# Layer kernel: gated unit and convolution tail placed between the last projection blocks, selection divided anew

## The chip, the cores and the metric

One core of one Trainium2 chip. The metric is the device time of one execution in microseconds, the median of the runs. Three runs of the kernel before gave 3154.9, 3154.71 and 3153.0 us, median 3154.71 us. The profiled execution took 3150.2 us, of which 3148.4 us lie between its first and last instruction (the span).

## The reference, cut to what matters

One pre-norm layer of a hybrid encoder, for 2048 prompt tokens and 32 sample tokens with 1024 cached keys. One projection of the normed input to 7748 columns feeds three branches, a gate path and merge gates:

```python
(aq, ak, av, iq, ik, iw, za, uv, zb, glu, zc, gates) = split_columns(rms_norm(x, norm_g) @ w_in)
# A: each query keeps the 256 best visible keys by an indexer score, then softmax attention over them
score = einsum('bths,bth->bts', relu(einsum('bthd,bsd->bths', iq, ik)), iw);  sel = top_k(score, 256)
# B: gmlp_unit
u, v = split(gelu(uv)); v = layer_norm(v, ln_g, ln_b)
o_b = u * (einsum('gij,bnjgc->bnigc', w_masked, v_chunks) + bs)        # chunks of 128 positions, 4 groups
# C: conv_module
c = a * sigmoid(g); y = causal_depthwise_conv31(c) + b; o_c = silu(layer_norm(y, ln_g, ln_b))
merged = ga*((o_a*silu(za)) @ w_a) + gb*((o_b*silu(zb)) @ w_b) + gc*((o_c*silu(zc)) @ w_c)
x = x + merged @ w_out;  x = x + sigmoid(rms_norm(x) @ w_pg) * (p @ w_ple);  y = rms_norm(x)
```

All of it is float32; matmuls run as three products of a high and a low part.

## The kernel before, in words

`STAGES` runs in this order on every engine: constants, trunk, gmlp, attend_loads, swish, turnover, attend, merge, finish.

**Trunk** (`stage_trunk`). The projection is cut into 61 jobs (`JOBS`) of 128 columns. A job is 5 spans of 416 tokens, a span is 8 slices (one for each 128 rows of the weights), a slice is 3 matmuls. After a span ScalarE copies or activates the PSUM bank into one of two buffers `j_out` and issues a store to `T_dram` (`evacuate`): five stores in a job. `high` (ScalarE) and `low` (GpSimd) split the next job's weights. Between these, ScalarE and GpSimd work through the depthwise convolution in 20 units (`make` and `add`), from job 9 on, spread over `CONV_JOBS` jobs by `CONV_TIMES`. From job 18 on one tile of keys and values a job is turned and stored (`natural_load`, `natural_store`).

**Selection** (`stage_select`), inside the trunk. The 256th best score of each row is found by bisection in two halves of 16 steps: the upper 16 bits, then the lower. For a tile in `DVE_TILES` VectorE does both (`whole`). For a tile in `ACT_TILES` VectorE prepares the keys (`offer`), ScalarE searches the upper half with sign sums (`Search.step`, L399), and VectorE does the rest (`complete`: waits for `found`, then `finish`, which ends at L455). The order on VectorE is written out by hand. When ScalarE takes a search step is fixed at build time by a planner in `scalar`: from the due time in `ACT_DUE`, whenever its running account of free time (`room`, from `JOB_US`, `EVACUATE_US`, `TAP_US`) covers half a step; at most half a job is saved up. The first step of a tile waits for `offer`. SyncE stores finished tiles and loads the next ones in the order of `FINISHED` and `LOADED`, and moves convolution units in between (`units`), also by planned times.

**Gmlp** (`stage_gmlp`) starts when all trunk stores and the selection are done. The values are loaded whole (`g_vT`), turned to token-major (L584), measured (L630), the mixing weights turned, then for each of 17 tiles: turned again, normed (L636), mixed (L600), shifted (L651), and GpSimd multiplies u by z (L697) and the result by that (L700). ScalarE's queue stores `g_ob`, two buffers.

**Swish** (`stage_swish`) works on the convolution's output `c.y`, loaded whole: for 5 spans of 422 columns, column sums by a ones matmul (L1362), centring (L1387), squares (L1417), sums of squares; then once over 2110 columns a square root, a reciprocal and one correction; then norm, silu and gate in 4 groups.

**Attend loads** put keys, values and the caches into rows of the attention's score buffer. SyncE issues them inside swish. **Turnover** waits for all engines and clears the semaphores. **Attend** first turns the cached keys, splits all operands into high and low (L1737, L1775), and TensorE starts on the first scores when every split is done (`operands`). The queries of tile 0 are loaded after the turnover and split by GpSimd (L1624 to L1628).

## Time and profile before

| stretch of the span, us | what | PE busy | granted clock |
|---|---|---|---|
| 0 to 1570.3 | trunk, 61 jobs | 80 to 100% of each 100 us or more | 0.97 to 1.00 |
| 1570.3 to 1776.6 | gmlp, swish, turnover | 80.4 of 206.3 | 0.73 |
| 1776.6 to 1799.7 | attention's operands | 3.3 of 23.1 | 0.57 |
| 1805 to 2352 | attention | 515.3 of 547.0 | 0.99 |
| 2352 to 2658 | merge | 277.1 of 306.0 | 0.94 |
| 2658 to 3148 | finish | 442.6 of 490.0 | 0.95 |
| 3148.4 | span | 2823.3 | 0.957 |
| 3150.2 | profiled execution | | |
| 3154.71 | median of three runs | | |

PE is TensorE. Busy is the time in which at least one matmul runs; granted clock is the share of full speed. The lines below name a source line, an engine, the tiles written and read, the shapes and how often. A bracket after a line of the timeline is the idle time before it and what ended it.

### The profile page before, as it was taken

What the parts mean: (1) busy time and instruction counts of PE and PEld (TensorE: products, weight loads), DVE (VectorE), ACT (ScalarE), POOL (GpSimd) and SP (SyncE); (2) the same over time, 40 slices, a digit from 0 to 9 for tenths busy, and PEclk for the clock granted to TensorE, in tenths of its full rate; (3) what the DMA queues carried; (4) which work ended last, traced back from release to release, by engine and by line L of the source; (5) the groups of instructions that cost most, each with busy time, mean ns of one, the idle gap of its engine ahead of it and who ended that gap; (6) DMA issues with size and microseconds to landing.
All of it is one profiled execution on the core that took longest, in us unless ns stands there. A gap on an engine that the chain in (4) does not pass through costs nothing. (4 is left out here: it accounts for less than half of the span.)

```text
span 3148.4 us, 43098 instructions
## 1 busy us (share of the span) xinstructions
PE 2823.3 (90%) x14677; PEld 2581.2 (82%) x14677; DVE 2302.5 (73%) x4035; ACT 1608.9 (51%) x2672; POOL 1342.9 (43%) x926
## 2 busy tenths in 40 slices
PE   6999999999999998898945189999988997799998
PEld 6999999999999998898942167778868897688886
DVE  7478947729999999999654778889976465465554
ACT  5375677877776767677201377777761001211111
POOL 1100477777888685676331254332213342111110
PEclk9999999999999999999987599999999998899999
DMA  4434233232333232232275332211016456311110
GB/s 152 127 130 154 69 105 106 91 121 92 104 114 103 82 121 83 76 108 67 89 239 134 116 74 55 67 54 41 30 35 218 152 161 216 97 65 65 65 65 34
DMA packets 293850, 321.07 MB, mean 102 GB/s; under 512 B 37537, under 2 KB 267681, under 8 KB 290077
## 3 DMA queue, kind: packets, MB, share of 16 engines
q1 hardware_dynamic: 158013, 180.90, 18.8%
q10 hardware_dynamic: 135648, 137.80, 13.2%
q8 instruction: 100, 1.64, 0.2%
q14 instruction: 89, 0.73, 0.1%
HBM read 194.46 MB, written 123.48 MB: 101 GB/s over the span
## 5 line engine op out<-in xcount | busy, mean ns | idle before, releaser
L1171 PE MATMUL psum<-hT_hi,j_whi 128*128 128x416 f32 x2440 | 868.1, 356 | 37.3 <-ACT j_out L1044 28.3
L1171 PE MATMUL psum<-hT_hi,j_wlo 128*128 128x416 f32 x2440 | 860.3, 353 | 0.0
L1171 PE MATMUL psum<-hT_lo,j_whi 128*128 128x416 f32 x2440 | 859.3, 352 | 0.0
L823 POOL TENSOR_TENSOR v_y<-v_y,v_product 128x422 f32<-128x422 f32 x580 | 721.1, 1280 | 246.9 <-ACT v_product L809 246.7
L1171 PEld LDWEIGHTS psum<-hT_hi,j_whi 128*128 128x128 f32 x2440 | 461.3, 189 | 54.2 <-ACT j_out L1044 32.8
L1171 PEld LDWEIGHTS psum<-hT_lo,j_whi 128*128 128x128 f32 x2440 | 462.5, 190 | 11.3
L1171 PEld LDWEIGHTS psum<-hT_hi,j_wlo 128*128 128x128 f32 x2440 | 461.6, 189 | 5.5
L416 DVE TENSOR_SCALAR_CACHE_REDUCE s_high<-s_key,s_cand 128x1024 int16<-128x1024 f32 (+4 forms) x240 | 392.9, 1637 | 8.4
L809 ACT ACTIVATE v_product<-v_x,v_taps 128x422 f32<-128x422 f32 x580 | 339.6, 640 | 74.2 <-POOL v_y L823 34.6
L1003 POOL TENSOR_TENSOR j_wlo<-j_w,j_whi 128x1024 fp32r<-128x1024 f32 x61 | 154.3, 2530 | 269.2 <-ACT j_whi L1036 269.1
L1803 DVE TENSOR_TENSOR a_ptlo<-psum,a_pthi 128x512 fp32r<-128x512 f32 x338 | 227.1, 681 | 45.3 <-ACT a_pthi L1752 44.8
L399 ACT ACTIVATE s_ajunk<-s_high,s_abias 128x2048 uint8<-128x2048 uint16 (+2 forms) x135 | 232.4, 1722 | 46.8 <-ACT j_out L1044 46.0
L1752 ACT ACTIVATE a_pthi<-psum 128x512 fp32r<-128x512 f32 x338 | 190.9, 595 | 111.6 <-PE psum L1687 110.1
L1044 ACT ACTIVATE j_out<-psum 128x416 f32<-128x416 f32 x305 | 153.2, 502 | 153.6 <-PE psum L1171 129.4
L1744 ACT ACTIVATE a_l<-a_l,a_lows 128x512 f32<-128x512 f32 (+4 forms) x136 | 183.7, 1351 | 38.1 <-DVE a_lows L1787 36.3
L1952 PE MATMUL psum<-m_ohi,m_whi 128*128 128x416 f32 x480 | 170.5, 355 | 30.1 <-POOL m_olo L1937 30.1
L1687 PEld LDWEIGHTS psum<-ident,a_l 128*128 128x128 f32 x1352 | 164.3, 140 | 40.6 <-ACT a_l L1744 4.4
L1713 PE MATMUL psum<-a_khi,a_qs 128*128 128x512 f32 x320 | 152.9, 478 | 47.0 <-DVE a_lows L1787 23.2
L1687 PE MATMUL psum<-ident,a_l 128*128 128x128 f32 x1352 | 192.5, 273 | 2.2 <-ACT a_l L1744 2.0
L2121 POOL TENSOR_TENSOR f_mhi<-f_mraw,zero 128x1024 fp32r<-128x1024 f32 x17 | 32.2, 1893 | 374.4 <-DMA f_mraw<-M_dram 333.9
L1952 PE MATMUL psum<-m_ohi,m_wlo 128*128 128x416 f32 x480 | 171.2, 357 | 0.0
L1952 PE MATMUL psum<-m_olo,m_whi 128*128 128x416 f32 x480 | 169.4, 353 | 0.0
(284 smaller groups left out, 5351.5 us busy)
## 6 DMA issues: line engine op xcount, KB each, us to landing
T_dram<-j_out ACTq DMA_DIRECT2D x305, 208.0 KB, 1.9
j_w<-in_w_in ACTq DMA_DIRECT2D x59, 512.0 KB, 4.1
m_gate<-T_dram SPq DMA_DIRECT2D x60, 416.0 KB, 3.5
m_oraw<-B_dram SPq DMA_DIRECT2D x15, 832.0 KB, 6.6
SC_dram<-i_acc SPq DMA_DIRECT2D x40, 256.0 KB, 2.0
M_dram<-m_merged ACTq DMA_DIRECT2D x5, 1664.0 KB, 10.4
n_x<-in_x_prompt SPq DMA_DIRECT2D x16, 512.0 KB, 4.6
a_q<-T_dram SPq DMA_DIRECT2D x32, 256.0 KB, 4.6
```

The costliest lines, as they stand in the source:

```text
L399: do(act.activation(a_junk[:, 0:n], high[HIGH_HALF[t]][:, 0:n], ACT.Sign, bias=bias, accum_out=a_cnt[:]))
L416: do(vec.tensor_scalar(junk, src, cand[:], 0.0, ALU.is_ge, ALU.add, accum_out=cnt[:]))
L809: act.activation(product[n % RING][:], x_in[:, k:k + CW_SPAN], ACT.Identity, scale=taps[:, k:k + 1]).then_inc(made, 1)
L823: pool.tensor_tensor(y[n % 2][:], y[n % 2][:], product[n % RING][:], ALU.add).then_inc(added, 1)
L1003: pool.tensor_tensor(w_lo[j % 2][:], w_raw[:], f32(w_hi[j % 2][:]), ALU.subtract).then_inc(w_lo_done, 1)
L1044: act.activation(out[r][:], c.psum[:, bank_of(j, b), 0:SPAN], FUNC[JOBS[j][2]]).then_inc(bank_read, 1)
L1171: last = pe.matmul(bank, w[p][:, k, :], h[:, k, t0:t0 + SPAN], start=(k == 0 and q == 0), stop=(k == KD - 1 and q == 2))
L1687: last = pe.transpose(c.psum[0:w, PT[u], r * P:(r + 1) * P], L[h][:, kt * P:kt * P + w], c.ident[:])
L1744: act.activation(L[h][:, 0:n], L[h][:, 0:n], ACT.Exp, bias=lows[:, h, lowest:lowest + 1], scale=-1.0, accum_out=sums[:, h:h + 1]).then_inc ...
L1752: act.activation(pT_hi[u][0:w, :], c.psum[0:w, PT[u], :], ACT.Copy).then_inc(pt_hi, 1)
L1803: vec.tensor_tensor(pT_lo[u][0:w, :], c.psum[0:w, PT[u], :], f32(pT_hi[u][0:w, :]), ALU.subtract).then_inc(pt_free[u], 1)
L1952: last = pe.matmul(c.psum[:, n, 0:SPAN], wt[:, b, k, n * P:(n + 1) * P], o[u][:, k, :], start=(k == 0 and q == 0), stop=(k == 3 and q == 2))
```

## The change

- `STAGES` is now constants, trunk, turnover, attend, merge, finish. Gmlp and swish are called inside the trunk: TensorE's part slice by slice from `span` (`gmlp.tensor_in`, `swish.tensor_in`), GpSimd's at the end of a job, ScalarE's after an evacuation, VectorE's after the selection, SyncE's after the selection's stores.
- Gmlp has a slice of its own for each step from job 56, span 4 (`GMLP_FROM`), swish a span for each half step from job 58, span 2 (`SWISH_FROM`). The values are loaded tile by tile into a ring of four, and twice. Stores go by SyncE. Swish takes its square root by `rsqrt` (14 small VectorE operations) for each span of 422.
- The attention gate's four silu jobs become the last four.
- Five stores of a job become two (`HELD`), from five buffers.
- Selection: 8 tiles for ScalarE, 7 for VectorE (tile DT goes over), in turn; new due times; `EVACUATE_US` 0.95 to 0.72; the convolution is spread over 47 jobs, not 49.
- Raw keys are loaded during swish, raw values and caches after its stores. Attention waits for fewer splits before its first score; the others follow (`splits` on VectorE in its first group, `late_split` on GpSimd before group 4).

Constants, the order of the jobs and the selection:
```diff
-        + [(col + s * P, slot + s, "silu") for col, slot in ((C_ZB, S_ZB), (C_ZC, S_ZC), (C_ZA, S_ZA)) for s in range(4)]
-        + [(C_G + s * P, S_G + s, "sigmoid") for s in range(24)])
+        + [(col + s * P, slot + s, "silu") for col, slot in ((C_ZB, S_ZB), (C_ZC, S_ZC)) for s in range(4)]
+        + [(C_G + s * P, S_G + s, "sigmoid") for s in range(24)]
+        + [(C_ZA + s * P, S_ZA + s, "silu") for s in range(4)])
...
-OUTS = 2
+HELD = [(0, 2), (2, 5)]
+GATED_UNIT_STORED = 29
+SWISH_GATE_STORED = 33
...
-CONV_FROM, CONV_JOBS = 9, 49
+CONV_FROM, CONV_JOBS = 9, 47
+GMLP_FROM, SWISH_FROM = (56, 4), (58, 2)
...
-JOB_US, EVACUATE_US, TAP_US, HIGH_US, SCORE_US = 22.8, 0.95, 0.66, 1.2, 0.455
+JOB_US, EVACUATE_US, TAP_US, HIGH_US, SCORE_US = 22.8, 0.72, 0.66, 1.2, 0.455
...
-ACT_TILES = [12, 13, 14, 15, 8, 9, 10, 11, DT]
-DVE_TILES = [4, 5, 6, 7, 2, 3]
-ACT_DUE = [32.0, 117.0, 212.0, 331.0, 546.0, 704.0, 846.0, 962.0, 1076.0]
-LOADED = [(12, 0), (4, 1), (13, 2), (14, 1), (15, 0), (5, 2), (8, 1), (6, 2), (9, 0), (7, 2), (10, 1), (2, 2), (11, 0), (3, 2), (DT, 1)]
-FINISHED = [(4, 98), (12, 193), (13, 311), (14, 453), (5, 529), (15, 610), (6, 686), (8, 753), (7, 829), (9, 895), (2, 945), (10, 1011),
-            (3, 1060), (11, 1125), (DT, 1169)]
-HIGH_HALF = {4: 0, 12: 1, 13: 0, 14: 1, 15: 0, 5: 1, 8: 1, 6: 0, 9: 0, 7: 1, 10: 1, 2: 0, 11: 0, 3: 1, DT: 1}
+ACT_TILES = [12, 13, 14, 15, 8, 9, 10, 11]
+DVE_TILES = [4, 5, 6, 7, DT, 2, 3]
+ACT_DUE = [30, 115, 277, 437, 595, 754, 870, 986]
...
-        whole(DVE_TILES[1])
-        for x in range(3, 7):
+        for x in range(len(ACT_TILES) - 1):
             offer(x + 1)
             complete(x)
-            whole(DVE_TILES[x - 1])
-        offer(8)
-        complete(7)
-        complete(8)
-    c.selected = [(early_stored, 32)] + [(s, 16 * sum(x == k for x in slot.values())) for k, s in enumerate(stored)]
+            if x + 1 < len(DVE_TILES):
+                whole(DVE_TILES[x + 1])
+        complete(len(ACT_TILES) - 1)
```
Gmlp, SyncE's part:
```diff
+    def sync(sp, rest_of_units):
+        c.wait_for_stored(sp, GATED_UNIT_STORED - 1)
+        c.wait_for_selected(sp)
...
+        def load_v(n):
+            t, r = n % TILES, n % RING
+            if n >= RING:
+                sp.wait_ge(turned, n - RING + 1)
+            sp.dma_start(vT[r][:, :, 0:real(t)], slot(S_GV, t)).then_inc(v_full[r], 16)
+        def load_uz(t):
+            p = t % 2
+            if t >= 2:
+                sp.wait_ge(gated, t - 1)
+            sp.dma_start(zT[p][:, :, 0:real(t)], slot(S_ZB, t)).then_inc(uz_full[p], 16)
+            sp.dma_start(uT[p][:, :, 0:real(t)], slot(S_U, t)).then_inc(uz_full[p], 16)
+        def store(t):
+            sp.wait_ge(gated, t + 1)
+            sp.dma_start(c.B_dram[1, :, :, at(t)].rearrange("s q t -> q s t"), ob[t % 2][:, :, 0:real(t)]).then_inc(stored[t % 2], 16)
+        for n in range(RING):
+            load_v(n)
+        load_uz(0)
+        load_uz(1)
+        rest_of_units(float("inf"))
+        for n in range(RING, TILES + RING):
+            load_v(n)
+        for t in range(TILES):
+            if TILES + RING + t < 2 * TILES:
+                load_v(TILES + RING + t)
+            store(t)
+            if t + 2 < TILES:
+                load_uz(t + 2)
+        sp.wait_ge(normed, TILES)
+        sp.dma_start(c.O["gmlp_sample"], vn[DT % 2][0:DEC].rearrange("q g n -> q (g n)")).then_inc(v_stored, 16)
+        sp.wait_ge(v_stored, 16)
+        for p in range(2):
+            sp.wait_ge(stored[p], 16 * len(range(p, TILES, 2)))
```
Gmlp, TensorE's part (`turn` turns four blocks of 128 by 128, `second` turns a tile again, after the norm of tile t - 2), and VectorE's and GpSimd's:
```diff
+    def mix(pe, t):
+        rows = real(t)
+        pe.wait_ge(normed, t + 1)
+        if t:
+            pe.wait_ge(mix_read, t)
+        for g in range(4):
+            last = pe.matmul(c.psum[:, MIX, g * P:(g + 1) * P], vn[t % 2][0:rows, g, :], wT[0:rows, g, :], start=True, stop=True)
+        last.then_inc(mixed, 1)
...
+        n = (j * len(SPANS) + b) * KD + k - first_slice
+        if 0 <= n < TILES:
+            if n == 0:
+                c.wait_for_natural(pe)
+            if n >= 3:
+                pe.wait_ge(measured, n - 2)
+            turn(pe, n, 5 + n % 3)
+        elif n == WEIGHTS_AT:
...
+        elif n == AGAIN_AT:
+            second(pe, 0)
+        elif AGAIN_AT < n <= AGAIN_AT + 2 * TILES:
+            t, odd = divmod(n - AGAIN_AT - 1, 2)
+            if odd:
+                mix(pe, t)
+            elif t + 1 < TILES:
+                second(pe, t + 1)
...
+        def shift(t):
+            p = t % 2
+            vec.wait_ge(mixed, t + 1)
+            if t >= 2:
+                vec.wait_ge(stored[p], 16 * (t // 2))
...
+        norm(0)
+        for t in range(TILES):
+            if t + 1 < TILES:
+                norm(t + 1)
+            shift(t)
...
+    def gates_in(pool, j):
+        for t in range(TILES):
+            if (first_slice + AGAIN_AT + 2 + 2 * t) // (KD * len(SPANS)) != j:
+                continue
+            p, w = t % 2, real(t)
+            pool.wait_ge(uz_full[p], 32 * (t // 2 + 1))
+            pool.tensor_tensor(uT[p][:, :, 0:w], uT[p][:, :, 0:w], zT[p][:, :, 0:w], ALU.mult).then_inc(multiplied, 1)
+            pool.wait_ge(multiplied, t + 1)
+            pool.wait_ge(mix_read, t + 1)
+            pool.tensor_tensor(ob[p][:, :, 0:w], ob[p][:, :, 0:w], uT[p][:, :, 0:w], ALU.mult).then_inc(gated, 1)
```
Swish:
```diff
+    def load_gate(sp, x):
+        if x:
+            sp.wait_ge(gated, x)
...
+    def sync(sp):
+        c.wait_for_moved(sp)
+        load(sp, 0)
+        load(sp, 1)
+        c.wait_for_gated(sp)
+        c.wait_for_stored(sp, SWISH_GATE_STORED - 1)
+        load_gate(sp, 0)
+        load(sp, 2)
...
+        x, odd = divmod(j * len(SPANS) + b - first_span, 2)
+        if (x, odd, k) == (X, 0, 0):
+            turn_tails(pe)
+        if not 0 <= x < X:
+            return
+        if not odd and k == 0:
+            if x == 0:
+                c.wait_for_mixed(pe)
+                pe.wait_ge(ones_made, 1)
+            else:
+                pe.wait_ge(centred, x)
+            pe.wait_ge(y_full[x % YS], 16 * (x // YS + 1))
+            total(pe, SUM, y[x % YS], summed)
+        if odd and k == 3:
+            pe.wait_ge(squared, x + 1)
+            if x >= 2:
+                pe.wait_ge(var_read, x - 1)
+            total(pe, 6 + x % 2, squares, var_summed)
...
+        def norm(x):
+            vec.wait_ge(var_summed, x + 1)
+            vec.tensor_scalar(var[:], c.psum[:, 6 + x % 2, 0:CW_SPAN], EPS, None, ALU.add).then_inc(var_read, 1)
+            vec.wait_ge(var_read, x + 1)
+            rsqrt(steps, rstd[:], var[:], tmp[:])
+            wide = rstd[:].unsqueeze(1).to_broadcast([P, 4, CW_SPAN])
+            vec.tensor_tensor(y[x % YS][:], y[x % YS][:], wide, ALU.mult).then_inc(normed, 1)
...
+        for x in range(X):
+            centre(x)
+            norm(x)
+            if x:
+                gate(x - 1)
...
+    def scalar_in(act, j, b):
+        x, odd = divmod(j * len(SPANS) + b - first_span, 2)
+        if 0 <= x < X and not odd:
+            act.wait_ge(centred, x + 1)
+            if x:
+                act.wait_ge(var_summed, x)
+            act.activation(squares[:], y[x % YS][:], ACT.Square).then_inc(squared, 1)
+        if odd and 0 <= x - 1 < X:
+            swish(act, x - 1)
```
Trunk:
```diff
-        select.sync(sp)
+        units = select.sync(sp)
+        gmlp.sync(sp, units)
+        swish.sync(sp)
+        load_keys.keys(sp)
+        swish.stores(sp)
+        load_keys.values(sp)
...
+            elif j == 2:
+                act.wait_ge(stored[r], 32)
+            else:
+                act.wait_ge(stored[1 if b < 2 else 4], 16 * j)
+            act.activation(out[:, r, :], c.psum[:, bank_of(j, b), 0:SPAN], FUNC[JOBS[j][2]]).then_inc(bank_read, 1)
+            if j < 2:
+                act.wait_ge(bank_read, q + 1)
+                act.dma_start(c.T_dram[slot, :, t0:t0 + SPAN], out[:, r, :]).then_inc(stored[r], 16)
+            elif b in (1, 4):
+                first, end = HELD[0 if b == 1 else 1]
+                act.wait_ge(bank_read, q + 1)
+                act.dma_start(c.T_dram[slot, :, first * SPAN:end * SPAN], out[:, first:end, :].rearrange("q b t -> q (b t)")
+                              ).then_inc(stored[b], 16)
...
-        while search.left():
-            search.step()
-        act.wait_ge(kv_stored, 32 * TILES)
+        assert not search.left()
+        wait_for_stored(act, SLOTS - 1)
```
Attention:
```diff
+            if group.n == 4:
+                for n in range(len(late_splits)):
+                    late_split(n)
...
+    splits = [(ks_hi[g][:, 0:PAST], ks_lo[g][:, 0:PAST], cacheT[g], (cache_turned, 1)) for g in range(KVH)]
+    splits += [(k_hi[g][:], k_lo[g][:], kraw[g][:], (k_full, 128)) for g in range(KVH)]
     for g in range(KVH):
-        splits += [(k_hi[g][:], k_lo[g][:], kraw[g][:], (k_full, 128)),
-                   (ks_hi[g][:, 0:PAST], ks_lo[g][:, 0:PAST], cacheT[g], (cache_turned, 1)),
-                   (ks_hi[g][:, PAST:], ks_lo[g][:, PAST:], new_k[g], (k_full, 128))]
-    for full, n, v, raw, rows, tiles in ((v_full, 16, v_p, vraw, P, slice(0, DT)),
-                                         (vs_full, 32, v_s, vsraw, P, slice(0, NV - 1)),
-                                         (vs_full, 32, v_s, vsraw, DEC, slice(NV - 1, NV))):
-        for g in range(KVH):
-            src, dst = raw[0:rows, tiles, g * HD:(g + 1) * HD], v[0:rows, tiles, g, :]
-            splits.append((dst[:, :, 0:HD], dst[:, :, HD:P], src, (full, n)))
+        for x in range(2):
+            dst = v_p[:, x * (DT // 2):(x + 1) * (DT // 2), g, :]
+            splits.append((dst[:, :, 0:HD], dst[:, :, HD:P], vraw[x][:, :, g * HD:(g + 1) * HD], (v_full, 32)))
+    FIRST_KEYS, FIRST_VALUES = KVH + 1, 2 * KVH + 2
...
-        pe.wait_ge(operands, 1)
...
+                if group.t == 0:
+                    pe.wait_ge(operands, FIRST_KEYS + group.g)
+                if group.t == DT:
+                    pe.wait_ge(late_ready, len(late_splits))
...
+            if group.n == 0:
+                for n in range(FIRST_KEYS, len(splits)):
+                    split(n)
```

## Rows read from the trace of the kernel before

**Rows 1.** Windows: length, PE, PEld, DVE, ACT, POOL busy, granted clock, DMA share, GB/s.
```profile
1570.30:1776.60 206.30, 80.39 (x377) 55.41 (x377) 105.80 (x154) 21.73 (x14) 41.86 (x35) 0.73 0.59 175
...
1620.00:1660.00 40.00, 18.57 (x140) 15.98 (x141) 22.14 (x59) 0.00 (x0) 28.82 (x24) 1.00 0.86 231
...
1660.00:1684.70 24.70, 5.28 (x22) 4.32 (x21) 7.54 (x16) 0.00 (x0) 7.74 (x8) 0.50 0.92 244
...
1776.60:1799.70 23.10, 3.26 (x16) 3.02 (x16) 20.57 (x12) 10.30 (x13) 17.35 (x14) 0.57 0.57 114
```
**Rows 2.** Timeline of PE: start and length in us, line, tiles, shapes, count.
```profile
1569.93 0.35 PE L1171 MATMUL psum<-hT_hi,j_wlo 128*128 128x416 f32 x1
...
1650.98 1.16 PE L600 MATMUL psum<-g_wT,g_vn 128*128 128x128 f32 x8 [1.43 <-DVE g_vn L636]
1651.98 0.60 PE L584 MATMUL psum<-ident,g_vT 128*128 128x128 f32 x4
...
1697.34 3.00 PE L1362 MATMUL psum<-g_y,w_ones 128*128 128x422 f32 x8
...
1799.74 0.80 PE L1713 MATMUL psum<-a_khi,a_qs 128*128 128x512 f32 x1 [19.89 <-DVEq L1776]
```
**Rows 3.** The page's part 5: the projection's weight loads.
```profile
L1171 PEld LDWEIGHTS psum<-hT_hi,j_whi 128*128 128x128 f32 x2440 | 461.3, 189 | 54.2 <-ACT j_out L1044 32.8
```
**Rows 4.** Waits from 300 to 1571 us: in total, times, longest.
```profile
DVE s_high L442 <- ACT s_afound L405: 141.8, 3, 60.4
...
ACT s_ajunk L399 <- DVEq L466: 47.6, 4, 15.9
```
**Rows 5.** Timeline of DVE in the selection: first finish, and ends of tiles.
```profile
446.76 1.61 DVE L442 TENSOR_SCALAR s_high<-s_high,s_afound 128x2048 bf16<-128x2048 uint16 x1 [42.05 <-ACT s_afound L405]
...
865.38 0.75 DVE L455 SCALAR_TENSOR_TENSOR s_key<-s_iota,s_qtail,s_key 128x512 f32<-128x512 int16 x1
...
947.67 1.47 DVE L455 SCALAR_TENSOR_TENSOR s_key<-s_iota,s_qtail,s_key 128x512 f32<-128x512 int16 x1
...
1028.16 1.48 DVE L455 SCALAR_TENSOR_TENSOR s_key<-s_iota,s_qtail,s_key 128x512 f32<-128x512 int16 x1
...
1186.35 0.75 DVE L455 SCALAR_TENSOR_TENSOR s_key<-s_iota,s_qtail,s_key 128x512 f32<-128x512 int16 x1
...
1250.41 1.46 DVE L455 SCALAR_TENSOR_TENSOR s_key<-s_iota,s_qtail,s_key 128x512 f32<-128x512 int16 x1
...
1546.75 0.75 DVE L455 SCALAR_TENSOR_TENSOR s_key<-s_iota,s_qtail,s_key 128x512 f32<-128x512 int16 x1
```
**Rows 6.** DMA issues in the gmlp and swish stages: KB each, median us to landing.
```profile
w_gate<-T_dram SPq DMA_DIRECT2D x4, 1040.0 KB, 6.8
...
g_uT<-T_dram SPq DMA_DIRECT2D x13, 256.0 KB, 3.8
B_dram<-g_ob ACTq DMA_DIRECT2D x13, 256.0 KB, 4.0
```
**Rows 7.** Timelines of POOL, DVE and ACT in the gmlp and swish stages.
```profile
1652.00 1.27 POOL L697 TENSOR_TENSOR g_uT<-g_uT,g_zT 128x512 f32<-128x512 f32 x1 [0.84 <-DMA g_uT<-T_dram]
...
1656.55 1.13 DVE L651 SCALAR_TENSOR_TENSOR g_ob<-psum,g_gain,g_offset 128x128 f32<-128x128 f32 x4 [1.70 <-DMA B_dram<-g_ob]
...
1690.70 1.91 DVE L1387 TENSOR_TENSOR g_y<-g_y,psum 128x1688 f32<-128x1688 f32 x1 [19.54 <-PE psum L1362]
...
1692.73 1.61 ACT L1417 ACTIVATE w_squares<-g_y 128x1688 f32<-128x1688 f32 x1 [121.90 <-DVE g_y L1387]
...
1738.75 2.36 DVE L1396 TENSOR_TENSOR w_tmp<-w_tmp,w_rstd 128x2110 f32<-128x2110 f32 x1
1741.14 1.26 DVE L1397 TENSOR_SCALAR w_tmp<-w_tmp 128x2110 f32<-128x2110 f32 x1
```
**Rows 8.** Timelines of SP and POOL after the turnover.
```profile
1776.55 0.67 SPq L159 DMA_DIRECT2D a_q<-T_dram  x1
...
1788.00 3.43 POOL L1628 TENSOR_TENSOR a_qs<-a_q,a_qs 64x1024 fp32r<-64x1024 f32 x1
```

574 lines of the change are left out of this document (278 added, 296 removed).

## The prediction

> **What bounds the kernel now.** I read the windows first, then TensorE's timeline, the waits, and VectorE's timeline through the selection. The reader is to see four things.
>
> The projection ends at 1570.3 us [rows 2]. From there to the attention's first scores at 1799.7 [rows 2] lie 229.4 us in which TensorE has little to do: 80.4 us busy of 206.3, then 3.3 of 23.1 [rows 1]. This is the only large stretch that the change can give back. Attention, merge and finish are not touched, so I move them as a block.
>
> The projection itself is TensorE's. A weight load takes 189 ns [rows 3] and is paced with its matmul, so a slice of three is 0.567 us, a span 4.54 and a job 22.7 us. Work put between slices adds its whole TensorE time, and every wait of TensorE there too, since TensorE takes its instructions in order.
>
> VectorE's selection ends at 1547.5 [rows 5], 22.8 us before the projection. 141.8 us of its length are three waits for ScalarE's searches, and ScalarE in turn waited four times for VectorE, 47.6 us in all [rows 4].
>
> Between 1620 and 1660 the gmlp stage is bound by neither compute engine: TensorE is busy 18.6 of 40 us, GpSimd 28.8, while the DMA engines are busy for 0.86 of it at 231 GB/s [rows 1]. A tile takes 3.45 us there. It is a ring of two buffers: a store lands after 4.0 us [rows 6], then VectorE's shift 1.13 and GpSimd's 1.27 [rows 7], plus 0.5 for the issue and hand-overs, 6.9 us for two tiles.
>
> **The change part by part.** I follow the moment at which TensorE can go on, from the selection to the first scores.
>
> *Selection.* With tiles in turn, VectorE no longer waits except for the first search, which ended at 446.8 [rows 5]. Its 16 steps are spread over spans by the planner's account; 0.23 us more room a span and one span earlier start bring the end to span 3 of job 12 from span 1 of job 13, three spans or 13.6 us. I take 432. From there VectorE works without a gap. Durations by differences of the ends of tiles [rows 5]: prepare one and complete one of 2048 keys 82.3 us (865.4 to 947.7), a whole tile of 1024 80.5 (947.7 to 1028.2), one of 1536 64.1 (1186.4 to 1250.4). A whole tile of 512 and one of 1056 lie around them; I take 63 and 76. Sum: 432 + 75 (finish tile 12) + 3 x 80.5 + 3 x 82.3 + 76 + 3 x 64 + 2 x 63 + 60 (last finish) = 1449. That is 98 us sooner than 1547.5. Without the first wait it would be 20 less; if ScalarE's late searches are not done in time, 15 more. ScalarE may still wait for `offer` around tiles 10 and 11 and hold TensorE up as now, but TensorE must then wait for the selection anyway: without any hold-up job 56, span 4 would begin near 1412, with those of before at 1462. So VectorE's chain sets the start, and lost projection time before it costs nothing.
>
> *Stores and room.* Three issues of a store fewer a job free ScalarE, about 1.2 us; the planner spends this on the searches. It is off the path: 0, bounds -5 and +3.
>
> *Start of gmlp.* SyncE stores the last tile (landing 3), issues four constants of 256 KB and the first values; landing behind them 6. I take 13 us: first turn at 1462. Bounds 8 and 20: before the last store SyncE also waits for the last convolution unit, which GpSimd should end near the same 1450.
>
> *Gmlp between slices.* It covers 61 slices, 34.6 us of projection. TensorE's own addition: 34 turns of four at about 0.5 (0.60 with its tail), 17 mixes of 1.0 [rows 2], with the constants 2: 36 us. But the waits decide. First pass: 17 turns, each needs 256 KB; with the gates' loads of 1 MB ahead of the fifth, at 231 to 270 GB/s, 24 us instead of 18. Nine slices without tiles and the small VectorE work: 7. Second pass: each mix waits for the shift before it, and that for a store two tiles back. Now the store, z and u are issued in a row by SyncE after GpSimd's product, so the ring is 0.15 + 3 x 0.37 issue + 4.3 landing + 1.27 + 1.27 + 0.3 = 8.4 us for two tiles, and the tile's DMA is 1024 KB where it was 768: at 231/0.86 = 269 GB/s at least 3.9 us. I take 4.5 us a tile (bounds 2.6, TensorE's own two slices, a turn and a mix, and 5.4, the DMA share of before scaled). 17 x 4.5 = 77. Together 24 + 7 + 77 = 108 us: last mix at 1570.
>
> *Start of swish.* It comes three slices later, but TensorE waits for `y_full`, and SyncE loads y only after the last tile is stored and `gmlp_sample` has landed. Last mix, shift and product 2.5, two landings of small stores 3.5, issue 0.5, y of 864 KB below the 6.8 of 1040 KB [rows 6], say 5.5: 12 us (bounds 8, 17). First column sum at 1582.
>
> *Swish.* Thirteen spans, 59.0 us. TensorE adds ten sums of 2.84 (3.00 with the tail [rows 2]) and 1.2 for the tails: 29.6. VectorE's loop is longer. Between one sum of squares and the next: `norm` (0.6 + 14 small operations on 422 columns, by the 2110-column rows 2.36/5 and 1.26/5 plus fixed parts [rows 7] about 0.5 and 0.3 each, 7.1 in all, + 1.91) = 9.6; `gate` 1.91; `centre` 1.91 [rows 7]; square 1.61 [rows 7]; the sum 2.84 and a slice boundary 0.5. That is 18.4 against TensorE's 2 x 4.54 + 2 x 2.84 = 14.8. The first sum of squares comes 9.7 after the start because the square is queued behind ScalarE's evacuation; four loops 73.6; 2.84 + five slices 2.84; tails 1.2; three spans 13.6: 104 us. Bound from below 90 if the loop is hidden, above 115. Projection ends at 1686, against 1570.3.
>
> *Turnover.* VectorE gates the last span just as TensorE ends; then store (landing 6), the tails' stores, and SyncE's issues of caches and values, about 7. Attention starts 15 us after the projection (bounds 10, 22): 1701. Before it was 206.3.
>
> *First scores.* Now the queries bound: q is issued at 1776.55 and its last split ends at 1791.43 [rows 8], 14.9 us. Keys and values were loaded before, and only three splits precede. I take 14. First score at 1715, against 1799.7. In the first group VectorE must still do five splits (2.3 + 4 x 1.1 us) before the first reciprocal: +6.5. GpSimd's six late splits, some 8 us, lie beside an attention in which TensorE is busy 94% and GpSimd a third: 0, at most +5.
>
> The move of the four silu jobs costs nothing: the same 61 jobs.
>
> Sum: 1799.7 - 1715 - 6.5 = 78 us saved. The profiled execution of 3150.2 becomes 3072; against the median of 3154.7, 4.5 us above it, 3077.
>
> By the clock: between 1620 and 1660, TensorE less than half busy with turns and mixes, the clock stayed at 1.00, that is at 2.4 GHz; between 1660 and 1684.7, busy a fifth, it was 0.50, at 1.2 GHz [rows 1]. In the changed gmlp phase TensorE is busy 2.6 us of 4.5, more than in the first of these. The Trainium skill (TensorE: Matmul & The Clock Gate, Part 4: PE-mode transpose) says that turning does not count as TensorE's activity for the clock; taken strictly, the second pass could run at 1.2 GHz. The first window speaks against it, the mixes being a part of it.
>
> **Rivals.**
> *Waits hidden.* The ring of stores and VectorE's loop in swish stay below TensorE's own work. Then gmlp takes 34.6 + 36 = 71 instead of 108, swish 92 instead of 104: another 49 us, 3028. For it: the stores of before landed in 4.0 with loads in between. Against it: GpSimd alone needs 2.54 a tile and its ring held TensorE idle half the time [rows 1]. Chance 0.14.
> *Late start or low clock.* The selection or the last convolution unit comes 20 us late, or the clock falls in the gmlp phase (slices 1.13, turns and mixes double: 5.2 a tile and 2.1 a turn, +24), or loads queue: 3098 to 3112. For it: ScalarE and VectorE wait for each other [rows 4] and the new due times leave 9 us. Chance 0.26.
> *The ring swallows it.* SyncE issues values, stores and gates in one order. If a landing of u or y is then two or three times 4 us, since all of it goes through one queue, each mix holds the whole projection. From 4.5 + 78/17 = 9.1 us a tile on, the change loses; at 10 us it is 3170. For it: 0.92 DMA share at 244 GB/s when other loads joined [rows 1]. Against it: 9.1 us are two landings in series and 1 MB needs 3.9. Chance 0.04.
> *It doesn't do what it says.* TensorE reaches span 4 of job 56 long before the selection, and all of gmlp and swish comes as late as now: within 0.2% of 3155. Chance 0.02.
>
> **How the numbers follow.** The forecast has 0.54 and its own range is 3052 to 3096 (the bounds of the terms, added as independent). The range of 8 in 10 reaches over most of the late case and a part of the hidden one: 3040 to 3112. A difference under 0.2%, 6 us, is what a measurement here cannot tell from none. Faster 0.94, same 0.02, slower 0.04.
>
> **What would show it.** The last L455 near 1449 with only one wait for `s_afound`; the first turn of gmlp at 1462; mixes 4.5 us apart, waiting for VectorE, that for `B_dram<-g_ob`; sums of squares 18.4 apart, waiting for ScalarE's squares; the last projection matmul at 1686; the first score at 1715. I am wrong if mixes follow each other every 2.6 us, if the projection before gmlp loses more than now, or if the turnover comes later than 22 us after the last slice.

## The result: 36 us faster, and where the other 42 went

Four executions of the changed kernel took 3114.23, 3118.1, 3117.54 and 3123.77 us, median 3117.82; the kernel before has a median of 3154.14 over four. The ratio is 0.9887, interval 0.987 to 0.9904: 36 us or 1.1% faster, beyond the noise, but less than half of the gain that I forecast (3077), and just above the range, whose end was 3112. The profiled execution took 3114.23 us, its span is 3112.2 against 3148.4.

The milestones, by the steps of the prediction:

| moment | predicted | measured | what lies between, predicted / measured |
|---|---|---|---|
| first cut of ScalarE found | 432 | 434.6 | |
| selection ends | 1449 | 1488.7 | 1017 / 1054.1 |
| first turn of gmlp | 1462 | 1500.5 | 13 / 11.8 |
| last mix | 1570 | 1597.2 | 108 / 96.7 |
| first column sum of swish | 1582 | 1608.2 | 12 / 11.0 |
| projection ends | 1686 | 1719.7 | 104 / 111.4 |
| attention's first turn | 1701 | 1737.9 | 15 / 18.2 |
| first score | 1715 | 1753.4 | 14 / 15.5 |

From the first score to the last instruction the changed kernel takes 10.2 us more than the one before (6.5 predicted). So 39.7 us of the miss stand before gmlp, and behind it -1.2 - 11.3 - 1.0 + 7.4 + 3.2 + 1.5 + 3.7 = +2.3 us.

TensorE's timeline, the lines that answer to [rows 2]:

```profile
1500.51 1.09 PE L603 MATMUL psum<-ident,g_vT 128*128 128x128 f32 x4 [16.60 <-DMA g_vT<-T_dram]
...
1536.17 1.09 PE L619 MATMUL psum<-g_wT,g_vn 128*128 128x128 f32 x8
...
1597.16 1.12 PE L619 MATMUL psum<-g_wT,g_vn 32*128 32x128 f32 x8 [3.09 <-DVEq L682]
1608.20 4.56 PE L814 MATMUL psum<-w_y,w_ones 128*128 128x422 f32 x6 [6.19 <-DMA w_y<-Y_dram]
...
1719.30 0.35 PE L1421 MATMUL psum<-hT_hi,j_wlo 128*128 128x416 f32 x1
1737.85 3.68 PE L1807 MATMUL psum<-ident,a_cache 128*128 128x128 f32 x16 [18.20 <-POOLq L2389]
1753.35 0.79 PE L1847 MATMUL psum<-a_khi,a_qs 128*128 128x512 f32 x1 [11.82 <-POOL a_qs L1741]
```

TensorE reached the first slice of the gmlp unit at 1483.9 and stood there for 16.6 us, because the values are loaded only after the last tile of the selection is stored. This wait takes the place of TensorE's idle time in the separate stages of before.

The waits from 300 to 1500 us (total, times, longest), which answer to [rows 4]:

```profile
DVE s_high L439 <- ACT s_afound L402: 42.4, 2, 31.0
ACT s_ajunk L396 <- DVEq L463: 32.5, 4, 17.4
...
PE psum L1452 <- DMA t_kvT<-T_dram: 20.7, 6, 7.5
...
PE psum L1421 <- ACT j_out L1288: 15.7, 3, 11.4
```

VectorE's wait for ScalarE fell from 141.8 to 42.4 us as intended: 31.0 for the first cut, and 11.4 for the last, which I had at zero. Windows of the gmlp stage's second pass, the swish and the turnover (columns as in [rows 1]):

```profile
1533.70:1598.30 64.60, 47.24 (x294) 39.95 (x293) 33.73 (x82) 3.12 (x5) 41.78 (x32) 0.95 0.89 245
1608.20:1719.70 111.50, 98.01 (x397) 77.35 (x397) 66.78 (x91) 27.91 (x39) 2.34 (x1) 0.92 0.43 134
1719.70:1737.90 18.20, 0.05 (x1) 0.05 (x1) 1.95 (x2) 0.51 (x1) 0.00 (x0) 0.56 0.90 233
```

TensorE was busy 80.4 of 206.3 us in the old stages [rows 1]; now it is 47.2 of 64.6 us in the second pass and 98.0 of 111.5 in the swish. DMA is as dense in the second pass as it was (0.89 at 245 GB/s against 0.86 at 231), in the swish it is not (0.43). The granted clock of the second pass is 0.95, near the upper level of 2.4 GHz: with projection slices between them, turns and mixes did not bring it down. Turns alone were not run.

### The profile page after: what moved, and what is told of

Read it like the earlier page. It is cut to its first block and busy times, and to the rows that moved or that the text cites. A ratio compares the mean times of both kernels' runs of the same rounds, so it can differ in the third digit from the quotient of the medians.

```text
span 3112.2 us, 42780 instructions
## 1 busy us (share of the span) xinstructions
PE 2835.6 (91%) x14677; PEld 2585.5 (83%) x14677; DVE 2343.5 (75%) x4162; ACT 1573.1 (51%) x2618; POOL 1369.7 (44%) x936
## 5 line engine op out<-in xcount | busy, mean ns | idle before, releaser
L1421 PE MATMUL psum<-hT_hi,j_whi 128*128 128x416 f32 x2440 | 880.2, 361 | 28.9 <-ACT j_out L1288 15.7
L1051 POOL TENSOR_TENSOR v_y<-v_y,v_product 128x422 f32<-128x422 f32 x580 | 737.2, 1310 | 197.3 <-ACT v_product L1037 197.2
L1421 PEld LDWEIGHTS psum<-hT_hi,j_whi 128*128 128x128 f32 x2440 | 464.5, 190 | 47.2 <-ACT j_out L1288 22.1
L413 DVE TENSOR_SCALAR_CACHE_REDUCE s_high<-s_key,s_cand 128x1024 int16<-128x1024 f32 (+4 forms) x240 | 393.0, 1637 | 8.4
L1241 POOL TENSOR_TENSOR j_wlo<-j_w,j_whi 128x1024 fp32r<-128x1024 f32 x61 | 161.7, 2651 | 321.0 <-ACT j_whi L1275 320.8
L396 ACT ACTIVATE s_ajunk<-s_high,s_abias 128x2048 uint8<-128x2048 uint16 (+1 forms) x120 | 214.1, 1784 | 13.2 <-ACT j_out L1288 12.1
L1880 ACT ACTIVATE a_l<-a_l,a_lows 128x512 f32<-128x512 f32 (+4 forms) x136 | 183.7, 1351 | 30.5 <-DVE a_lows L1929 28.8
```

The source lines that it names most:

```text
L396: do(act.activation(a_junk[:, 0:n], high[HIGH_HALF[t]][:, 0:n], ACT.Sign, bias=bias, accum_out=a_cnt[:]))
L413: do(vec.tensor_scalar(junk, src, cand[:], 0.0, ALU.is_ge, ALU.add, accum_out=cnt[:]))
L1051: pool.tensor_tensor(y[n % 2][:], y[n % 2][:], product[n % RING][:], ALU.add).then_inc(added, 1)
L1241: pool.tensor_tensor(w_lo[j % 2][:], w_raw[:], f32(w_hi[j % 2][:]), ALU.subtract).then_inc(w_lo_done, 1)
L1421: last = pe.matmul(bank, w[p][:, k, :], h[:, k, t0:t0 + SPAN], start=(k == 0 and q == 0), stop=(k == KD - 1 and q == 2))
L1880: act.activation(L[h][:, 0:n], L[h][:, 0:n], ACT.Exp, bias=lows[:, h, lowest:lowest + 1], scale=-1.0, accum_out=sums[:, h:h + 1]).then_inc ...
```

## The experiments

All edits are to the changed kernel unless another is named. "Selection's end" is the end of the last tile's L452, "the stretch" the time from the first turn of gmlp (L603) to attention's first turn (L1807): 237.3 us in the changed kernel. Each run has one profile, so such moments are those of one execution; medians are over all executions. The runs were made on several chips, each beside the kernel before, whose medians lie between 3153.2 and 3156.0; the ratios allow for that, differences of medians do not.

**The start follows the selection.** First, both units (gmlp and swish) start a span later.

```diff
-GMLP_FROM, SWISH_FROM = (56, 4), (58, 2)
+GMLP_FROM, SWISH_FROM = (57, 0), (58, 3)
```

> The changed kernel with the gated unit's slices and the swish's slices both one span of the projection later (GMLP_FROM (57, 0), SWISH_FROM (58, 3)). In the changed kernel TensorE reached the unit's first slice at 1483.9 us and waited 16.6 us there. Theory A (TensorE's own idle time sets the end): the wait shrinks by one span, 4.6 us, and the total by 4 to 5 us, to about 3109.5 us. Theory B (VectorE's chain from the end of selection to the swish's last gate sets the end, TensorE follows): the first turn of a tile stays within 2 us of 1500.5, the last projection matmul comes some 4 us earlier, the turnover stays near 1737.5, and the total moves by less than 1.5 us.

Ratio 0.9904 (0.9887 to 0.992), median 3124.0. TensorE's wait did not become a gain: it is 14.0 us instead of 16.6, and the stretch is 238.4 us. Selection ended 5.9 us later (1494.6), although nothing in it was changed, and the first turn (1506.8) moved with it. So theory B's chain holds and A fails; B's own numbers, a first turn within 2 us of 1500.5 and a total within 1.5, were missed mostly by these 5.9 us, whose cause is an instruction shown below.

```diff
-            search(K, e, 1)
+            search(K, e, 1, 1)      # the last of 16 steps left out
```

(`search` gets a fourth argument for it, 0 elsewhere.)

> The changed kernel with the last of the 16 steps of the low-half search left out in each of the 15 searched tiles (the cut found is then off by one step). A step is 2.35 us at 2048 keys, 1.81 at 1536, 1.28 at 1024, 0.75 at 512 and about 0.6 us of small instructions: 34 us less on VectorE in all. Theory A (VectorE's chain is what was late, and it also held TensorE back, because ScalarE stood 29.7 us in front of tiles that VectorE had not offered yet and read out no banks meanwhile): TensorE reaches the unit's first slice 15 to 30 us before 1483.9, the first turn comes 20 to 34 us before 1500.5, and the total falls by 18 to 34 us. Theory B (TensorE is late by stalls of its own): TensorE still reaches the slice at about 1484, the wait of 16.6 us goes and nothing more, total 12 to 17 us shorter. Theory C (ScalarE's last search sets the end of selection): its end stays near 1436, selection ends only some 3 us sooner and the total falls by 3 us.

0.9825 (0.9803 to 0.9847), median 3100.2. Selection ended at 1469.9, the first turn came at 1482.3, 18.2 us sooner, and the total fell by 17.6. That is theory A, though just under its ranges (20 and 18 us), for of 34 us less work only 19 arrived in selection's end. TensorE reached the first slice at 1465.2, 18.7 us sooner. What is gained in selection's end reaches the total nearly one to one.

**What made the selection long.**

```diff
-            pool.tensor_tensor(y[n % 2][:], y[n % 2][:], product[n % RING][:], ALU.add).then_inc(added, 1)
+            half = CW_SPAN // 2
+            pool.tensor_tensor(y[n % 2][:, 0:half], y[n % 2][:, 0:half], product[n % RING][:, 0:half], ALU.add).then_inc(added, 1)
```

> The changed kernel with GpSimd's 560 additions of the convolution over half of their columns (the other half of each product is left out of the sum). One add of 128x422 takes 1.31 us; half should take about 0.7, so GpSimd is some 340 us less busy between 320 and 1440 us. Theory A (VectorE's slow tiles come from work beside GpSimd): pieces of selection fall from 83.0 and 86.7 us per tile to about 80.5 and 82.3 us as I had summed, the single instructions that took 1555 ns (128x512 multiply of the tops) and 1421 ns (signs) fall to about 1080 and 990 ns, selection ends 20 to 30 us sooner, total 15 to 25 us shorter. Theory B (the sizes of the pieces were summed wrongly and GpSimd has no part in them): pieces change by less than 1 us, total by less than 5 us, from ScalarE's waits for the adds alone (52.5 us).

0.9674 (0.9657 to 0.9691), median 3053.3: 64.6 us less, three times what I expected. (This kernel leaves out half of the convolution's sum, so its result is not the layer's.) Selection ended at 1428.9, 60 us sooner, though VectorE now waits 41 us for the last cut. VectorE's groups between 320 and 1440 us, of the changed kernel and then of this run:

```profile
L413 DVE TENSOR_SCALAR_CACHE_REDUCE s_high<-s_key,s_cand 128x2048 int16<-128x2048 f32 x64 | 150.2, 2346 | 2.2
L450 DVE TENSOR_SCALAR s_key<-s_iota,s_qfrom 128x512 f32<-128x512 int16 x37 | 47.2, 1275 | 1.3
L426 DVE TENSOR_SCALAR s_high<-s_key 128x1024 int32<-128x1024 int32 x14 | 21.4, 1530 | 0.1
```

```profile
L413 DVE TENSOR_SCALAR_CACHE_REDUCE s_high<-s_key,s_cand 128x2048 int16<-128x2048 f32 x64 | 150.2, 2347 | 2.2
L450 DVE TENSOR_SCALAR s_key<-s_iota,s_qfrom 128x512 f32<-128x512 int16 x40 | 29.6, 740 | 1.4
L426 DVE TENSOR_SCALAR s_high<-s_key 128x1024 int32<-128x1024 int32 x14 | 15.2, 1089 | 0.1
```

The searching instruction (L413) costs the same to a nanosecond; the others pay for GpSimd's additions. Adding up, for each line and form, the time above the shortest instruction of that line and form, from 300 to 1550 us, gives 128 us in the kernel before, 127 in the changed one, 70 here. So the price is large, but it was in the kernel before as well.

```diff
-            for x, (a, w) in enumerate(pieces(n)):
-                do(vec.tensor_scalar(K[:, a:a + w], iota[:, 0:w], -1.0, q_from[:, x, t:t + 1], ALU.mult, ALU.add))
+            for a in range(0, n, WIDE):          # WIDE = 1536, iota_wide has as many columns
+                w = min(WIDE, n - a)
+                do(vec.tensor_scalar(K[:, a:a + w], iota_wide[:, 0:w], -1.0, q_from[:, a // PIECE, t:t + 1], ALU.mult, ALU.add))
```

> The changed kernel with an iota of 1536 instead of 512 columns, so that the distances of a tile are written by one or two instructions instead of up to four: 21 instead of 46 over the searched tiles (the junk row of tile 16 lies on the buffers of the k and v tiles, long done by then). In the changed kernel this instruction took from 0.49 to 1.67 us for the same 512 columns, 30.4 us above its shortest in all, and the run with half of the additions cut that to 10.8 us. Theory A (each such instruction waits for an addition of GpSimd's under way, a price per instruction rather than per column): VectorE's chain shortens by 15 to 25 us and the total by as much. Theory B (the price is per column: both engines share the bandwidth while they overlap): 512 columns cost the same in a wide instruction, VectorE gains 0 to 5 us, and so does the total.

(The wide row needs room: the junk row of tile 16 moved onto other buffers, with a wait for those in front of that tile.) 0.9831 (0.9815 to 0.9848), median 3101.6, 16.3 us less, which is A's number. Selection ended at 1476.6, 12.1 us sooner; the rest lies behind it. Its groups:

```profile
L453 DVE TENSOR_SCALAR s_key<-s_iota,s_qfrom 128x1536 f32<-128x1536 int16 x7 | 13.5, 1923 | 0.2
L453 DVE TENSOR_SCALAR s_key<-s_iota,s_qfrom 128x1024 f32<-128x1024 int16 x4 | 5.9, 1476 | 0.1
L453 DVE TENSOR_SCALAR s_key<-s_iota,s_qfrom 128x512 f32<-128x512 int16 x6 | 5.8, 967 | 0.2
```

1536 columns cost 1.92 us where three pieces cost 3.8 (3 x 1.275): the price beside additions is mostly per instruction.

**The instructions of 6 to 22 us.** In the profile of every kernel without gaps, the one before included, but not in the one with half additions, VectorE had one to three of them, scans (L446, 5.2 to 6.6 us) left aside. They are always L439 or L445 (by the changed kernel's lines), the first full-width instructions after a search. The largest, in the run with two Newton rounds (below), and GpSimd beside it:

```profile
883.09 22.14 DVE L439 TENSOR_SCALAR s_high<-s_high,s_cand 128x1024 bf16<-128x1024 uint16 x1
905.26 2.00 DVE L440 SCALAR_TENSOR_TENSOR s_key<-s_key,s_high 128x1024 f32<-128x1024 uint16 x1
```

```profile
880.42 14.77 POOL L1051 TENSOR_TENSOR v_y<-v_y,v_product 128x422 f32<-128x422 f32 x14
895.16 2.39 POOL L1241 TENSOR_TENSOR j_wlo<-j_w,j_whi 128x1024 fp32r<-128x1024 f32 x1
897.52 7.43 POOL L1051 TENSOR_TENSOR v_y<-v_y,v_product 128x422 f32<-128x422 f32 x7
905.02 1.16 POOL L1055 TENSOR_TENSOR v_yout<-v_y,v_y 128x422 f32<-128x422 f32 x1
```

It began beside a row of 14 additions and lasted through the subtraction (L1241) and seven more. It ended at 905.23; GpSimd's row had ended at 904.95 and its next instruction began 0.07 us later. In the run a span later L439 took 17.57 us for tile 16, 16.1 more than in the changed kernel's profile; tile 16 ended 12.6 us later there, and the next piece gave 6.8 us back: that is its late selection. The other form did not help:

```diff
-            do(vec.tensor_scalar(above, H[:, 0:n], threshold, 65536.0, off, ALU.mult))
+            do(vec.scalar_tensor_tensor(out=above, in0=H[:, 0:n], scalar=threshold, in1=factors[:, 0:1].to_broadcast([P, n]), op0=off, op1=ALU.mult))
```

(and the same for `is_equal`, L445)

> The changed kernel with two of VectorE's instructions in each finish (the shift of the upper half to bfloat16, and the comparison for equality into int16) written as scalar_tensor_tensor with a constant as second tensor, the same result. In the runs so far single ones of just these two took 6 to 22 us instead of 0.5 to 1.6 (22.14 us in one run, 17.57 in another, 8.2 in nearly all), each time beside a chain of GpSimd's additions without a gap, and none did with the additions halved. Theory A (this form of instruction is kept out as long as GpSimd has additions in a row, others only for one addition): no instruction of VectorE except scans takes over 4.5 us in selection; the new forms cost about 1 us more each at 2048 keys, 15 us in all, so selection ends between 5 us sooner and 8 us later than 1488.7, the runs scatter less. Theory B (any instruction of VectorE can be hit): others of 6 to 20 us appear, and selection ends 15 us later.

0.9982 (0.9965 to 0.9999), median 3144.8: a miss of theory A, and the nine executions scatter more, not less (3136.7 to 3161.5). The same two places still took 9.06 and 7.39 us, no others did (so not B either), and the new form costs more everywhere: at 2048 keys 2.81 us on average in L439's place, where it was 1.21, and 2.91 in L445's, where it was 1.59. Selection ended at 1516.0. A second form at the same places is hit as well; whether the place alone decides was not tested. Then gaps for GpSimd:

```diff
-                pool.wait_ge(added, u * ADDED + (n - 1))
+                pool.wait_ge(added, u * ADDED + n)
```

> The changed kernel with every addition of GpSimd's chain waiting for the addition just before it to be complete, instead of the one before that, so that a small gap stands after each (the sums are the same). In the changed kernel additions in a row follow each other every 1.06 us without a gap. Single instructions of VectorE took 6 to 22 us beside them, always the first full-width ones after a search, in whichever form; each ended within 0.2 us of the last addition of a row. Theory A (VectorE gets in only where GpSimd leaves a gap): no instruction of VectorE apart from scans takes over 4.5 us; selection ends 10 us or more before the usual 1489 to 1506, near 1470 to 1480, and the total is 3098 to 3112 us. Theory B (the gap makes GpSimd's chain longer, ScalarE wait for it, and so TensorE): selection ends as before or later and the total is 3120 us or more. Theory C (gaps do not matter; the first instruction after a search is slow for another reason): 6 to 20 us instructions stay.

> As the run with a gap after each addition, but a gap only after every fourth. Theory A: a starved instruction waits for at most four additions, 4.3 us, so none takes over 6 us; other instructions stay as in the changed kernel; selection ends 5 to 12 us before the usual, total 3103 to 3114 us. Theory B and C: as in the run with a gap after each; under B this one costs a quarter of that one.

(for the second, `n` where `n % 4 == 0`, else `n - 1`.) Gap after each: 0.9884 (0.9869 to 0.9899), median 3119.4; after every fourth: 0.986 (0.9845 to 0.9875), 3113.0. The mechanism of A is borne out: L439 and L445 took at most 3.13 us, nothing but scans more than 4.4. The gain is not: selection ended at 1497.1 and 1491.4, and the time above the shortest is 131 and 125 us, about the 127 of the changed kernel. What the long ones no longer take, the short ones do. So these instructions move selection's end from one profile to the next, by 5.9 us in the run a span later, but they are not the miss. That they make the scatter of the executions is not shown here: it is 6.9 and 8.2 us with gaps against 9.5 without.

**ScalarE's side.**

```diff
-ACT_DUE = [30, 115, 277, 437, 595, 754, 870, 986]
+ACT_DUE = [30, 115, 284, 437, 595, 768, 892, 1002]
```

> The changed kernel with four of ScalarE's eight searches due later (tile 14 by 7 us, 9 by 14, 10 by 22, 11 by 16), so that ScalarE is not sent in front of a tile that VectorE has yet to offer. In the changed kernel it stood there four times, 32.5 us in all, and read out no banks meanwhile. Theory A (VectorE's chain sets the start of the units, and projection time lost before it costs nothing): the four waits shrink below 10 us in sum, TensorE reaches the unit's first slice 10 to 25 us earlier and waits there as much longer than 16.6 us, and selection's end and the total stay as they are, within what the starved instructions of VectorE scatter them (some 8 us). Theory B (these waits are what the missing time is): the total falls by 15 us or more.

0.992 (0.9905 to 0.9935), median 3128.9: slower by 11 us, neither theory. TensorE did wait 37.1 us at the first slice, 20.5 more than in the changed kernel, but it got there no sooner (1487.3). ScalarE's waits stayed at 30.2 us; two instructions of 17.58 and 16.66 us (L439) held VectorE up, and selection ended at 1511.9. The profiled execution (3138.1) is the slowest of the four; the others took 3128.1 to 3129.3, so some 10 us of the loss have no profile. That a late selection moves the total is seen once more: the stretch is unchanged (236.9). Whether later due times help without such a mishap is not shown.

```diff
+        whole(DVE_TILES[-1])        # tile 3, now between complete(10) and complete(11)
         complete(len(ACT_TILES) - 1)
```

(with the last whole tile left out of the loop, the key buffers of tiles 3 and 11 exchanged and tile 11 due 54 us earlier)

> The changed kernel with the last tiles in another order: tile 11 is offered to ScalarE before tile 10 is completed, VectorE's own tile 3 comes after that, and tile 11 is completed last as before; tile 11's search is due 54 us earlier, tiles 11 and 3 exchange key buffers. In the changed kernel VectorE waited 11.45 us for the last cut. Theory A (this wait is in the chain that starts the units): it goes, selection ends 9 to 13 us sooner (near 1477), the first turn still 12 us behind it, total 8 to 13 us shorter. Theory B (TensorE cannot be at the unit's first slice before 1484, and ScalarE's denser searching takes away from the projection what VectorE gains): the first turn comes at 1495 or later and the total falls by less than 5 us.

0.9879 (0.9863 to 0.9896), median 3116.2: 1.7 us less, B's number but not its reason, since TensorE still waits 15.1 us at the first slice. The wait for the last cut is gone, and VectorE waits for no other engine after the first cut; but from the end of tile 9 to selection's end it takes 183.7 us instead of 187.9, and a 13.1 us instruction (L439, tile 16) came before. The prepare of tile 11 now falls beside additions and takes 10.6 us instead of 5.1, and other instructions are moved beside them too. Of 11.45 us of waiting 4.2 arrived.

**The kernel before with the new selection alone** (tile lists, junk row, due times, `EVACUATE_US`; the scratch for DMA descriptors is halved to 4096 bytes to make room).

> The kernel before with nothing changed but the selection: tiles alternate between ScalarE and VectorE as in the changed kernel, tile 16 is searched by VectorE with a junk buffer of its own, ScalarE's due times and evacuation cost are those of the changed kernel (and the scratch for DMA descriptors is 4096 bytes, to make room). Theory A (the new order of selection shortens VectorE's chain, but in the kernel before the projection ends last): selection ends near 1450 to 1490 instead of 1546.75, the last projection matmul stays between 1560 and 1575 (1569.93 before), and the total changes by less than 10 us either way. Theory B (the long search on ScalarE was what held back the last projection jobs as well): the projection ends 20 to 30 us sooner, and so does the kernel, so that selection alone carries most of the 36 us.

1.0055 (1.0038 to 1.0072), median 3172.4: slower by 16.6 us, and both theories wrong. Selection ends 41.7 us sooner (1505.8), but the projection ends 18.9 us later (1588.8). TensorE's waits from 300 to 1500 us are, before and here:

```profile
PE psum L1171 <- ACT j_out L1044: 28.3, 7, 9.6
PE psum L1200 <- DMA t_kvT<-T_dram: 10.3, 3, 6.4
PE psum L1171 <- POOL j_wlo L1003: 4.3, 4, 2.1
```

```profile
PE psum L1163 <- ACT j_out L1036: 22.2, 10, 11.5
PE psum L1163 <- POOL j_wlo L995: 17.1, 8, 5.3
PE psum L1192 <- DMA t_kvT<-T_dram: 14.7, 5, 6.3
```

That is 11 us more; the rest I cannot assign. One candidate was not tested: the planner's `EVACUATE_US` of 0.72 belongs to two stores a job, and this kernel still issues five, so ScalarE may be sent to search when it should read out banks. TensorE's waits for ScalarE's read-outs came 10 times instead of 7 but are shorter in sum; those for GpSimd's split of the weights, which follows ScalarE's, grew from 4.3 to 17.1 us. What the run shows is that an earlier selection alone gains nothing, because in the kernel before the projection ends last.

**The swish's loop.**

```diff
-            rsqrt(steps, rstd[:], var[:], tmp[:])
+            rsqrt(steps, rstd[:], var[:], tmp[:], 2)      # rounds, 3 before
```

> The changed kernel with two rounds instead of three in the swish's inverse square root (4 of VectorE's 14 small instructions a tile left out, in the swish alone; the result is less exact). In the changed kernel the sums of squares stand 20.5 us apart, 5 of them; a round is 0.60 + 0.60 + 0.38 + 0.60 us and the steps between, 2.32 us. Theory A (from the end of selection on VectorE's chain sets the time, and every microsecond of the swish's loop counts five times): the loop falls to 18.2 us and the total by 10 to 12 us. Theory B (TensorE's projection spans fill the loop in any case): the loop stays at 20 us and the total within 2 us.

0.9874 (0.9852 to 0.9896), median 3117.2, as much as the changed kernel. But selection ended 16.8 us late (1505.5, with the 22 us instruction), and the stretch is 221.5 us, 15.8 shorter. ScalarE's squares of the changed kernel and then of this run:

```profile
1634.96 1.61 ACT L894 ACTIVATE w_squares<-w_y 128x1688 f32<-128x1688 f32 x1 [2.08 <-DVE w_y L857]
1655.46 1.61 ACT L894 ACTIVATE w_squares<-w_y 128x1688 f32<-128x1688 f32 x1 [3.85 <-DVE w_y L857]
1675.97 1.61 ACT L894 ACTIVATE w_squares<-w_y 128x1688 f32<-128x1688 f32 x1 [3.85 <-DVE w_y L857]
```

```profile
1649.68 1.62 ACT L894 ACTIVATE w_squares<-w_y 128x1688 f32<-128x1688 f32 x1 [0.47 <-ACT j_out L1288]
1666.20 1.61 ACT L894 ACTIVATE w_squares<-w_y 128x1688 f32<-128x1688 f32 x1 [1.54 <-DVE w_y L857]
```

20.5 us apart against 16.5 (the others 15.4 to 19.1). The swish's loop behaves as theory A has it, and more; the total does not, for the selection was late. 2.3 us less work took more than that from the loop; I read this as the sums' fixed slices, of which a later one is caught or missed, but did not test it.

```diff
+        centre(0)
         for x in range(X):
-            centre(x)
-            norm(x)
+            if x + 1 < X:
+                centre(x + 1)
             if x:
                 gate(x - 1)
+            norm(x)
```

> The changed kernel with VectorE's order in the swish turned: the next tile is centred, and the last one gated, before a tile is normalised, so that the mean, the squares and their sum of tile x+1 run under the inverse square root of tile x. Theory A (the loop of 20.5 us is a chain through four engines, of which VectorE's own work is 9.6 + 3 x 1.9 = 15 us): the loop falls to 15 to 16 us, the swish ends 15 to 25 us sooner, total 15 to 25 us shorter. Theory B (loads and stores of the three y buffers, or ScalarE waiting in order for the normalised tile, take the place of the chain): the loop stays over 19 us and the total falls by less than 8 us.

0.9889 (0.9854 to 0.9924), median 3112.0; three executions took 3107.3 to 3112.0, two 3130.9 and 3131.5, of which there is no profile, so a gain over the changed kernel is not established. Squares 15.5, 15.5, 19.1 and 17.6 us apart: A at first, then TensorE waits for the loads of y (12.9 us, 3 times), B. The stretch is 227.3 us, 10.1 shorter; selection ended at 1494.7.

**Together.** Two rounds, centred ahead, the swap and the wide iota; then with the other form, and with gaps.

> The changed kernel with the four edits of the last runs together: two Newton rounds in the swish, the last tiles swapped, the next tile centred ahead in the swish, the wide iota. Singly they took from selection's end some 4 us (swap), 12 to 17 us (iota), and from the stretch between the first turn and the attention's first turn 15.8 us (Newton rounds: 221.6 against 237.4) and 10.2 us (centred ahead: 227.2). Theory A (selection's chain and the swish's loop are separate terms of one sum): selection ends near 1470, the stretch is 215 to 220 us, and the total is 3075 to 3092 us. Theory B (once VectorE is ahead, TensorE's own spans or the loads of y take the place of the loop): the stretch stays at 221 to 227 us and the total is 3092 to 3100 us.

> The kernel of the four edits together and, in addition, the two instructions of VectorE that were starved written in the other form. Theory A (they cost on average as much as they save, but take the scatter away): within 5 us of the kernel with four edits, with a narrower spread from run to run. Theory B (starvation is the larger part): 8 to 15 us faster than that kernel.

> The kernel of the four edits together (3084.2 us; it had instructions of 21.8 and 10.3 us) with the gap after each addition. Theory A: selection ends at 1450 to 1460 instead of 1480.7 and the total is 3055 to 3070 us. Theory B: 3085 us or more. It also tells whether TensorE can follow: it reached the first slice at about 1472 in that kernel, so with selection's end at 1455 the first turn would come at 1472 or later, not at 1467, unless ScalarE's shorter waits let TensorE be there sooner.

> The kernel of the four edits together with the gap after every fourth addition. Theory A: between the kernel of the four edits and the one with the gap after each, 3065 to 3078 us. Theory B: within 3 us of 3084.

| run | ratio to before | median | selection's end | stretch | first turn to end of span |
|---|---|---|---|---|---|
| changed kernel | 0.9887 (0.987 to 0.9904) | 3117.8 | 1488.7 | 237.3 | 1611.7 |
| four edits | 0.979 (0.977 to 0.9809) | 3084.2 | 1480.7 | 221.1 | 1598.2 |
| and other form | 0.9868 (0.9853 to 0.9883) | 3112.8 | 1503.0 | 220.9 | 1595.3 |
| and gap after each | 0.9782 (0.9769 to 0.9796) | 3086.8 | 1477.6 | 222.4 | 1599.3 |
| and gap after every fourth | 0.9771 (0.9758 to 0.9785) | 3083.1 | 1470.3 | 221.0 | 1598.1 |

The last is the fastest kernel here, 34.7 us below the changed kernel and 73 below the one before. Its five executions lie within 2.7 us, those with a gap after each within 4.8, those of the four edits without gaps within 15 (3083.2 to 3098.2): here the gaps buy evenness, not time, theory B in both runs. (TensorE reached the first slice of the four edits at 1482.3, not at the 1472 of the expectation.) The other form made the kernel 28.6 us slower, which neither theory had. With both swish edits the stretch is no shorter than with two rounds alone (221.5): theory B for the stretch, A for the total. The profiled execution of the four edits took 3092.7 us and had instructions of 21.8 and 10.3 us, so its 1480.7 stands for a slower one than the median. First turn and first score of the fastest kernel:

```profile
1482.41 1.09 PE L609 MATMUL psum<-ident,g_vT 128*128 128x128 f32 x4 [11.70 <-DMA g_vT<-T_dram]
...
1718.52 0.80 PE L1855 MATMUL psum<-a_khi,a_qs 128*128 128x512 f32 x1 [11.45 <-POOL a_qs L1749]
```

The last column of the table is the strongest reading: over the changed kernel and all nine runs of it with its swish left as it was, whatever was changed before it, first turn to the end of the span is 1610.0 to 1613.9 us, while the first turn itself lies anywhere from 1441.2 to 1528.0, 11.8 to 12.5 us behind selection's end.

## Why the prediction was wrong, step by step

- **The mechanism held.** VectorE's chain sets the start and TensorE waits for it (13 to 37 us in the runs with the old swish): the runs with the units a span later, a step less and half the additions show it. So did the first cut (432, 434.6), the 13 us from selection's end to the first turn (11.8) and the 12 us to the swish (11.0).
- **The step that failed is the selection's sum, "= 1449".** By its own terms, with what they measured in brackets: finish of tile 12 75 (72.9); three whole tiles of 1024 keys at 80.5 (82.1 to 83.2, together +6.8); three pieces of 2048 at 82.3 (86.1 to 86.7, +12.2); tile 16 at 76 (87.0, +11.0); three pieces of 1536 at 64 (72.6, 65.2, 65.3, +11.1); two whole tiles of 512 at 63 (61.1 and 58.5, -6.4); last finish 60 (11.45 of waiting and 52.65, +4.1); start +2.6. The tile 16 term was an error of my own making: it has 1056 keys and is searched in both halves, so it cannot cost less than the 80.5 of a tile with 1024. The others were single rows [rows 5] used as constants, and the cheap ones of their kind. The 82.3 was moreover read from start to start of the two last instructions; from end to end it is 83.0.

Ends of tiles in the kernel before that [rows 5] leaves out:

```profile
782.75 1.48 DVE L455 SCALAR_TENSOR_TENSOR s_key<-s_iota,s_qtail,s_key 128x512 f32<-128x512 int16 x1
...
1099.48 1.47 DVE L455 SCALAR_TENSOR_TENSOR s_key<-s_iota,s_qtail,s_key 128x512 f32<-128x512 int16 x1
...
1313.87 0.75 DVE L455 SCALAR_TENSOR_TENSOR s_key<-s_iota,s_qtail,s_key 128x512 f32<-128x512 int16 x1
...
1377.96 1.47 DVE L455 SCALAR_TENSOR_TENSOR s_key<-s_iota,s_qtail,s_key 128x512 f32<-128x512 int16 x1
...
1437.35 1.47 DVE L455 SCALAR_TENSOR_TENSOR s_key<-s_iota,s_qtail,s_key 128x512 f32<-128x512 int16 x1
```

And ends of tiles in the changed kernel (tiles 15, 16, 8, 2, 9 and 11):

```profile
1013.40 1.48 DVE L452 SCALAR_TENSOR_TENSOR s_key<-s_iota,s_qtail,s_key 128x512 f32<-128x512 int16 x1
...
1100.44 1.48 DVE L452 SCALAR_TENSOR_TENSOR s_key<-s_iota,s_qtail,s_key 128x512 f32<-128x512 int16 x1
...
1173.01 1.48 DVE L452 SCALAR_TENSOR_TENSOR s_key<-s_iota,s_qtail,s_key 128x512 f32<-128x512 int16 x1
...
1234.82 0.75 DVE L452 SCALAR_TENSOR_TENSOR s_key<-s_iota,s_qtail,s_key 128x512 f32<-128x512 int16 x1
...
1299.32 1.48 DVE L452 SCALAR_TENSOR_TENSOR s_key<-s_iota,s_qtail,s_key 128x512 f32<-128x512 int16 x1
...
1487.93 0.75 DVE L452 SCALAR_TENSOR_TENSOR s_key<-s_iota,s_qtail,s_key 128x512 f32<-128x512 int16 x1
```

By kind, from end to end:

| piece | taken | all in the kernel before | in the changed kernel |
|---|---|---|---|
| whole tile of 1024 keys | 80.5 | 81.9, 80.5, 86.2 | 83.0, 82.1, 83.2 |
| prepare and complete, 1536 | 64 | 71.3, 64.8, 64.8 | 72.6, 65.2, 65.3 |
| complete of 2048 without a wait | 82.3 | 83.0 | 86.7, 86.4, 86.1 |
| whole tile of 512 keys | 63 | 62.8, 59.4 | 61.1, 58.5 |
| tile 16, 1056 keys | 76 | searched in another way | 87.0 |

So most of the miss was on record before the change: the means of the rows before (82.9 and 67.0 for the first two kinds) would have added 7.1 and 8.9 us, where 6.8 and 11.1 were missing. Only the pieces of 2048 keys became dearer, by some 3 us each (two of the three also prepare 2048 keys, where the one of before prepared 1536).

What these pieces consist of is shown by the run with half the additions: the same instruction costs by what GpSimd does beside it, about 5 us a tile between full and half additions (83.0 to 78.0 for tile 5). The prepare of a tile of 1536 keys took 11.9 us beside additions (tile 9, from 1101.84) and 5.1 where GpSimd paused (tile 10, from 1235.49).

Windows of the two tiles of 1024 keys, before ([rows 5], the 80.5) and after:

```profile
949.20:1029.70 80.50, 80.50 (x429) 79.71 (x428) 76.47 (x150) 54.47 (x96) 67.61 (x56) 1.00 0.34 111
```

```profile
845.60:928.80 83.20, 78.91 (x412) 77.27 (x411) 79.16 (x151) 53.54 (x95) 70.83 (x56) 0.98 0.38 123
```

VectorE's busy time (fourth figure) is 2.7 us longer for nearly the same instructions, GpSimd's (sixth) 3.2. The changed kernel packs the convolution into 47 jobs instead of 49, but the rows do not bear out that this density is what the sum lacks. Here are the third tile of this kind in the kernel before and the one piece of 2048 keys there, then a piece of 2048 keys in the changed kernel:

```profile
1100.90:1187.10 86.20, 86.20 (x459) 85.25 (x458) 82.16 (x151) 51.06 (x93) 70.64 (x59) 1.00 0.35 112
866.10:949.10 83.00, 83.00 (x444) 82.08 (x443) 80.43 (x90) 64.33 (x119) 68.57 (x47) 1.00 0.35 108
```

```profile
928.80:1014.90 86.10, 86.10 (x459) 85.03 (x458) 83.53 (x90) 66.48 (x121) 66.19 (x44) 1.00 0.24 80
```

The third tile had GpSimd busy for 70.6 us, as much as the one of the changed kernel, and took longer (two of the long instructions, 7.28 and 6.15 us, are in it). In the piece of 2048 keys GpSimd is busy for 66.2 of 86.1 us where it was 68.6 of 83.0. The whole tiles of 1024 average 82.9 us before and 82.8 after. What makes the pieces of 2048 keys dearer, the phase between the two engines or something else, stays open, and so does a small part for the density; a run with 49 jobs was not made.

The Trainium skill (SBUF — State Buffer, SBUF: two separate sides) says that VectorE and GpSimd share a pair of ports as a lock held for the whole instruction, which only some forms of VectorE's instructions need.
- **"If ScalarE's late searches are not done in time, 15 more"** was named as a bound and left out of the value: VectorE waited 11.45 us for the last cut.
- **TensorE's arrival was misread too.** The prediction has job 56, span 4 begin near 1412 without hold-ups and near 1462 with those of before. Counting the projection's matmuls, it began at 1471.9 in the kernel before, and TensorE stood at this place at 1483.9 in the changed one. So a selection ending at 1449 could not have given a first turn at 1462 unless TensorE had come sooner by as much. It does come sooner with an earlier selection (1465.2 with a step less, 1428.0 with half the additions), so the two are coupled; what an end at 1449 alone would have given is not shown.
- **The swish's loop** was put at 18.4 us and measured 20.5, 104 against 111.4 us in all. The 14 small operations took 0.60 and 0.38 us each, 7.8 together where 7.1 was taken; and from the end of the square (1657.07) to VectorE's read of the sum of squares (1661.95, L861) it is 4.9 us, where 2.84 and 0.5 were taken. That the sum waits there for its fixed slice fits the run with two rounds, whose loop shrank by more than its work, but was not tested.
- **Gmlp** was too dear: a tile 4.0 us (from 1533.7 to 1597.2 for 16), not 4.5. The ring fits as the cause (between 1533 and 1600 VectorE waited 25.2 us for the store of `g_ob`, TensorE 14.9 for VectorE), but the store landed in 2.9 us where I took 4.3:

```profile
B_dram<-g_ob SPq DMA_DIRECT2D x16, 256.0 KB, 2.9
```

- **Turnover, first score, first group** were each 1.5 to 3.7 us too cheap; attention's queries bound as said (TensorE waits 11.8 us for `a_qs`). None of this was tested.
- **The rival "late start" (0.26)** is what came, at its place, but the selection was 40 us late where it said 20, and the total lies 6 us above its 3098 to 3112. That the total is not further off is partly luck: gmlp was 11.3 us cheaper than forecast and paid for the swish and the turnover. Its low clock did not come. "Waits hidden" did not come (a tile 4.0 us, not 2.6), and neither did "The ring swallows it", which needed more than 9.1.

## What to carry to other kernels

When the bound moves to another engine, price each piece of that engine's chain by the mean of all its rows, not by one of them: here three whole tiles of 1024 keys took 80.5, 81.9 and 86.2 us, and the lowest went into the sum three times. Look up how long the other engines need to reach the same place, too. Find the one moment through which everything must pass (here the end of the selection) and measure its distance to the end; if that distance is constant over edits that precede it, what precedes and what follows can be worked on apart. Beside a busy GpSimd, try fewer and wider instructions on VectorE before less work.

## What the runs showed of the hardware that I had not expected

- An instruction of VectorE stood for 22.14 us and ended within 0.3 us of a gap of 0.07 us between GpSimd's instructions; it happened only to the first full-width one after a search (6 to 22 us), and in two forms. With each addition waiting for the one before it there was none of these (at most 3.13 us at these places), at no cost in time (3119.4 against 3117.8).
- VectorE's searching instruction with a sum as its result is untouched by GpSimd (2346 and 2347 ns at 2048 keys); writing 512 columns (L450) takes 1.28 us on average beside the additions where its shortest is 0.48.
- Halving the width of 580 additions of 1.3 us, on an engine that waits 197 us for another (ScalarE's products, 300 to 1500 us), made the kernel 64.6 us faster.
